# Moving rows of the three-product maps read last column first on one core

## The reference

```
# first block, 272 tokens
proj = rmsnorm(h) @ w_in            # 2048 x 4112
... gated linear attention (4 heads), multi-scale pooling ...
h = h + mixed @ w_out               # 2048 x 2048
z = rmsnorm(h) @ mlp_w1             # 2048 x 8192
h = h + square(relu(z)) @ mlp_w2    # 8192 x 2048
# second block, 256 tokens
proj = x @ w_in_2                   # 2048 x 9552
... two attentions (8 heads each), a gate ...
x = layer_norm(ALPHA * x + merged @ w_out_2)
x = layer_norm(ALPHA * x + mem_cross_attention(x, mem))
g, u = split(x @ w_ffn_in)          # 2048 x 11264
x = layer_norm(ALPHA * x + (silu(g) * u) @ w_ffn_out)   # 5632 x 2048
```

## Time and profile before

| | |
|---|---|
| time, median of 3 runs | 2574.3 us (2574.04 to 2575.87) |
| span of the profiled execution, first to last instruction | 2573.8 us |
| mean granted TensorE clock in it | 0.998 |
| TensorE matmul busy | 2555.9 us, 99%, 15948 instructions |
| VectorE busy | 1572.9 us, 61% |
| ScalarE busy | 1189.7 us, 46% |
| HBM read | 464.93 MB, 181 GB/s over the span |

### The profile page before, as it was taken

How to read it: one execution, slowest core, us unless ns; L and a number is a source line. 1 busy time by engine, 2 the same in 40 slices (tenths; PEclk the granted TensorE clock), 3 DMA queues, 4 the chain that set the end, 5 groups by cost and what they waited for, 6 DMA issues and landing times.

```text
span 2573.8 us, 41371 instructions
## 1 busy us (share of the span) xinstructions
PE 2555.9 (99%) x15948; PEld 2297.6 (89%) x15948; DVE 1572.9 (61%) x2178; ACT 1189.7 (46%) x1609; POOL 27.9 (1%) x70
## 2 busy tenths in 40 slices
PE   9999999999999999999999999999999999999998
PEld 7999988888888888899999999988999888888886
DVE  5444856556556555565565566666876776656665
ACT  5543545434444344544444454444544445445442
POOL 1000000000000000000000000000000000000000
PEclk9999999999999999999999999999999999999999
DMA  7664556666555665574455565565576577567753
GB/s 251 179 180 130 165 181 180 196 196 186 190 184 191 196 195 186 173 224 154 131 165 170 160 200 183 186 213 161 150 205 180 189 196 191 189 186 186 195 196 114
DMA packets 467782, 468.80 MB, mean 182 GB/s; under 512 B 9246, under 2 KB 384142, under 8 KB 466862
## 3 DMA queue, kind: packets, MB, share of 16 engines
q1 hardware_dynamic: 465600, 459.31, 58.5%
q0 software_dynamic: 2064, 7.82, 0.9%
HBM read 464.93 MB, written 2.10 MB: 181 GB/s over the span
## 4 chain that ended last, share of the span: by engine, by line
PE 97%; DVE 1%; ACT 1%; DMA 0%; issue 0%; SPq 0%; DVEq 0%; ACTq 0%
PE ps L693 17%; PE ps L696 11%; PE ps L697 11%; PE ps L698 11%; PE ps L725 11%; PE ps L727 11%; PE ps L726 11%; PE ps L694 9%; PE ps L789 1%; DMA region<-in_mem 0%; PE ps L1130 0%; PE ps L1101 0%; DVE w_lo L2091 0%; PE ps L1137 0%; PE ps L1173 0%; PE ps L1006 0%
## 5 line engine op out<-in xcount | busy, mean ns | idle before, releaser
L2091 DVE TENSOR_TENSOR w_lo<-raw,w_hi 128x1024 fp32r<-128x1024 f32 (+1 forms) x867 | 1047.5, 1219 | 766.0 <-ACT w_hi L1438 764.5
L1438 ACT ACTIVATE w_hi<-raw 128x1024 fp32r<-128x1024 f32 (+1 forms) x869 | 902.1, 1051 | 909.4 <-PE ps L727 410.1
L693 PE MATMUL ps<-xa,w_hi 128*128 128x512 f32 x1920 | 666.0, 391 | 0.0
L696 PE MATMUL ps<-xa,w_hi 128*128 128x256 f32 (+2 forms) x2112 | 607.4, 288 | 0.0
L698 PE MATMUL ps<-xa,w_lo 128*128 128x256 f32 (+2 forms) x2112 | 595.0, 282 | 0.0
L697 PE MATMUL ps<-xa,w_hi 128*128 128x256 f32 (+2 forms) x2112 | 593.4, 281 | 0.0
L694 PE MATMUL ps<-xa,w_lo 128*128 128x256 f32 x1920 | 537.3, 280 | 0.0
L693 PEld LDWEIGHTS ps<-xa,w_hi 128*128 128x128 f32 x1920 | 360.1, 188 | 79.6
L697 PEld LDWEIGHTS ps<-xa,w_hi 128*128 128x128 f32 x2112 | 398.4, 189 | 2.0 <-issue 1.0
L696 PEld LDWEIGHTS ps<-xa,w_hi 128*128 128x128 f32 x2112 | 397.2, 188 | 3.2 <-issue 2.0
L698 PEld LDWEIGHTS ps<-xa,w_lo 128*128 128x128 f32 x2112 | 396.5, 188 | 0.0
(11 more groups left out here) (364 smaller groups left out, 2537.0 us busy)
## 6 DMA issues: line engine op xcount, KB each, us to landing
raw<-in_mlp_w SPq DMA_DIRECT2D x128, 1024.0 KB
raw<-in_w_in SPq DMA_DIRECT2D x106, 1024.0 KB
raw<-in_w_ffn_in SPq DMA_DIRECT2D x176, 512.0 KB
raw<-in_w_ffn_out SPq DMA_DIRECT2D x44, 1024.0 KB
raw<-in_w_out SPq DMA_DIRECT2D x32, 1024.0 KB
raw<-in_w_o_dsa SPq DMA_DIRECT2D x8, 1024.0 KB
raw<-in_w_o_moba SPq DMA_DIRECT2D x8, 1024.0 KB
raw<-in_w_kv_mem SPq DMA_DIRECT2D x7, 1024.0 KB
```

The lines of the kernel that those rows point to most:

```text
L693: nc.tensor.matmul(o, hi, x.rearrange("p a n -> p (a n)"), start=opens and ci == 0, stop=False)
L696: nc.tensor.matmul(o, hi, x_hi, start=opens and ci == 0, stop=False)
L1438: return nc.scalar.activation(dst, src, ACT.Copy, **kw)
L2091: V.tensor_tensor(w_lo[:, ps_ % CUT, 0:n], raw[:, bs % RAW, n * half:n * half + n], w_hi[:, ps_ % CUT, 0:n].bitcast(F32), ALU.subtract).th ...
```

## The change

A helper returns a view with its last dimension reversed, and every three-product matmul gets it for its moving operand and for its output. Column n of the moving row still lands in column n of the bank; both are walked from the last column to the first. The stationary operands, the small steps, the order of the instructions, their number, the waits and the buffers stay as they are.

```diff
+            def down(v):
+
+                return v[:, ::-1]
...
-                                    nc.tensor.matmul(o, hi, x.rearrange("p a n -> p (a n)"), start=opens and ci == 0, stop=False)
-                                    ins = nc.tensor.matmul(o[:, 0:SEQ], lo, x_hi, start=False, stop=closes and ci == 3)
+                                    nc.tensor.matmul(down(o), hi, down(x.rearrange("p a n -> p (a n)")), start=opens and ci == 0, stop=False)
+                                    ins = nc.tensor.matmul(down(o[:, 0:SEQ]), lo, down(x_hi), start=False, stop=closes and ci == 3)
                                     continue
-                                nc.tensor.matmul(o, hi, x_hi, start=opens and ci == 0, stop=False)
-                                nc.tensor.matmul(o, hi, x_lo, start=False, stop=False)
-                                ins = nc.tensor.matmul(o, lo, x_hi, start=False, stop=closes and ci == 3)
+                                nc.tensor.matmul(down(o), hi, down(x_hi), start=opens and ci == 0, stop=False)
+                                nc.tensor.matmul(down(o), hi, down(x_lo), start=False, stop=False)
+                                ins = nc.tensor.matmul(down(o), lo, down(x_hi), start=False, stop=closes and ci == 3)
...
-                        nc.tensor.matmul(o, x_hi, hi, start=opens and ci == 0 and seed is None, stop=False)
-                        nc.tensor.matmul(o, x_hi, lo, start=False, stop=False)
-                        ins = nc.tensor.matmul(o, x_lo, hi, start=False, stop=closes and ci == len(chunks) - 1)
+                        nc.tensor.matmul(down(o), x_hi, down(hi), start=opens and ci == 0 and seed is None, stop=False)
+                        nc.tensor.matmul(down(o), x_hi, down(lo), start=False, stop=False)
+                        ins = nc.tensor.matmul(down(o), x_lo, down(hi), start=False, stop=closes and ci == len(chunks) - 1)
```

More of the change, by code:

```diff
@@ L1394, in _ @@
                         x_hi, x_lo = lhs(c, tb)
-                        nc.tensor.matmul(o, x_hi, hi, start=False, stop=False)
-                        nc.tensor.matmul(o, x_hi, lo, start=False, stop=False)
-                        ins = nc.tensor.matmul(o, x_lo, hi, start=False, stop=k == 7 and ci == 1)
+                        nc.tensor.matmul(down(o), x_hi, down(hi), start=False, stop=False)
+                        nc.tensor.matmul(down(o), x_hi, down(lo), start=False, stop=False)
+                        ins = nc.tensor.matmul(down(o), x_lo, down(hi), start=False, stop=k == 7 and ci == 1)
                 ins.then_inc(half_done, 1)
```

## The result

The changed kernel takes 2623.94 us in the median of three runs (2623.90 to 2624.23), the kernel before 2574.3 us. The ratio is 1.0191 with a 95% interval of 1.0173 to 1.0209: **slower by 49.6 us**. The time lies inside the predicted range, but the forecast, no change, was wrong.

A forecast was written before the change was run, and what follows sets the result against it. TensorE's matmul spacing was taken to bound the kernel. The terms summed 0 + 0 + 0 + 0 + 0, giving 2574 us, the median of the runs before, with a range of 2520 to 2680 us.

The forecast's parts named there:

- What bounds the kernel: Whole span: TensorE busy 99%, hardly waiting, so every nanosecond of matmul spacing shows; 189 us of gap could be won.
- rival D: Dense matmuls: opposed direction breaks up the pattern of slower matmuls, the gap shrinks; -30 us, 2544 us; chance 0.22.
- Parts 1 and 2: Instructions, waits, semaphores, buffers and DMAs unchanged; banks complete and are read as before; cost 0 each.
- Part 3: Accumulation in a bank: closest distance between two writes of one column stays 256 columns; cost 0.
- part 4: `row_product` writes upward before a reversed matmul adds to the same bank, 16 times; taken 0, at most 6 us.
- Part 5: Streaming rate of the 15,072 dense matmuls: taken 0, bounds -30 us and +2090 us.
- Rival A: Dense matmuls: the gap does not see the direction; 2574 us, within 5 us; chance 0.36.
- Rival B: Dense matmuls: backward rows meet loads of the next stationary tile worse, gap grows 5 ns; 75 us, 2650 us; chance 0.27.
- Rival C: Dense matmuls: the fast stream holds only upward, each column costs 0.84 ns; +2090 us, 4660 us; chance 0.15.

The follow-up runs named there:

- write_down: Against the kernel before: only the bank is written from last column to first, moving rows read upward, in all three forms; 2575.44 us, ratio 1.0002.
- up_shift: The kernel before, reading upward, with every row of activations moved 4 columns down; 2607.55 us, ratio 1.0125.
- up_edge6: The kernel before, reading upward, with only xh, xf, xm and xk moved to 6 columns past a multiple of 16; 2591.99 us, ratio 1.0067.
- up_edge2: The kernel before, reading upward, with only xh, xf, xm and xk moved to 2 columns past a multiple of 16; 2585.49 us, ratio 1.0041.

## Why the prediction was wrong

- **What bounds the kernel**: right. TensorE was busy 99% and hardly waited, and the nanoseconds added to the spacing are the time lost. (VectorE's casts in rival D's argument are 1047 us by the busy time of the earlier trace rows; 867 x 1.219 would be 1057, since the row's mean is not that of all its forms. Nothing hangs on it.)
- **Parts 1 and 2** (instructions, waits, reads of the banks): right, cost 0.
- **Part 3 and part 4** (distance between writes, `row_product` upward before a downward write): `write_down` has both and its ratio is 1.0002 (0.9992 to 1.0011). Cost 0, as taken, to some 3 us.
- **Part 5, the streaming rate: this step failed.** It was set to 0 "because place makes no difference to the mean in the earlier trace rows". Those rows are of the narrow form, with two placements that happen to agree, and placement says nothing of direction by itself. In the broad form, which carries a third of the time, reading downward costs 8 ns a matmul, and 4 columns of placement (`up_shift`) or 2 (`up_edge6`) are worth 5 ns reading upward. Even in the narrow form the agreement was luck: with 258 columns `up_shift` takes 0.1201 us where the kernel before takes 0.1179, in the mean. The two rows were one pair of placements of one form and were taken for a rule over all of them. The same part had noted that the gap "sits in a pattern that repeats and can settle at another level", and that was the better lead, though only half of its evidence holds: the wide pairs do alternate, and the narrow ones have two levels, but the 0.230 and 0.226 us of the broad form come from stretches of five matmuls; over whole stages `xh` has 0.2285 and `xm` 0.2284 us. Its term should have been +3.3 ns on average and was 0; its upper bound of +2090 us was far too wide.
- **Rival A**, no change, had the largest chance (0.36) and gave the forecast; the spacings moved by ten times its 0.34 ns.
- **Rival B** has the sign, 50 us where it was priced at 75, 3.3 ns a matmul in the mean and not 5. Its chance was 0.27. Its mechanism, a gap that depends on how the walk of the row meets the load of the next tile, is supported for the broad form by `up_edge2` and `up_edge6`, in which only the tile moved. Its argument against itself, that broad and narrow have about the same gap, was empty: the two answer to the change quite differently, 8 ns and 0 to 2 ns. The signs the prediction had named, the same nanoseconds in all three forms or twice as much in 512 columns as in 256, both failed with it: it was 8 ns for a broad matmul, 6.7 ns for a wide pair of two matmuls, and nothing (`xo`) to 2 ns for a narrow one. That both streams read the same memory and hinder each other there was not measured; the runs show the dependence, not the place where the time passes.
- **Rival C**, the halved stream, is out: 512 descending columns take 0.2366 us, not twice 0.213. The Trainium skill (Advanced Engine Details and Errata, PSUM Cachelines) warns that a non-contiguous pattern slows matmuls significantly; for a bank written downward `write_down` shows a ratio of 1.0002, so the strict reading does not hold for a step of -1. The result agrees with its next sentence, on two consecutive elements, but no run here parts two such elements, so that one is not tested.
- **Rival D**: the opposed walk did break up the pattern of the earlier trace rows, but to the longer of its two values and not to the shorter.
- What stays open: which rule gives the levels 0.2283, 0.2333 and 0.2367 us. Three simple ones (difference of the two places, kind of the first group read, place of the activations) were each contradicted; theory G was not, but it gives spans and no levels. Nor is it known what chooses between the two levels of the narrow form, or why the wide form is slower downward wherever its rows were put. A stationary tile read the other way was not tried.

## What to carry to other kernels

Where TensorE is the bound and rows stream densely, the placement of the stationary tile and of the moving row by 16 bytes, and the direction of the row's walk, can be worth time: here the slowest of the kernels took 1.9% more than the fastest. Read upward and measure the placement for each form apart, since no rule found here carries over from one form to another. The order in which a bank is written, upward or downward, made no difference here. Before setting an effect to zero because two rows agree, ask whether they are of the form that carries the time: 15,072 matmuls turn 0.34 ns into a measurable difference.

## What was not expected of the hardware

A move of 4 columns of the activations alone, with no other edit, costs the upward kernel 32 us (ratio 1.0125). A row read in groups of 4 columns from the last to the first costs as much as the full reversal, 0.2367 us, in groups of 16 less, 0.2333 us, and in groups of 128 nothing (at the placement of this kernel). A stage of narrow matmuls went from 0.1187 to 0.1167 us in its middle, after its last small step, with the same lines, rows and placement. And the level 0.2333 us comes back in most of the placements and in both directions, as if it were what a broad matmul takes when neither a good nor a bad meeting applies; that is a guess.
